# Applying the rms factor of an even block where its projections are read, with the first projection in halves

## What is computed

```python
def rmsnorm(x, g):
    y = xf * lax.rsqrt(jnp.mean(xf * xf, axis=-1, keepdims=True) + EPS)
    return (y * g).astype(x.dtype)

def even_mixer(h, w_in, lb, hg_norm_g, ret_norm_g, w_out):      # h = rmsnorm(x, g[0])
    p = (h @ w_in).astype(jnp.float32)
    hq, hf, hi, hgate, rq, rk, rv, rgate = jnp.split(p, splits, axis=-1)
    f = lb + (1.0 - lb) * jax.nn.sigmoid(hf)
    o_hg = hgrn2_scan(silu(hq), 1.0 - f, jnp.log(f), hi)        # in chunks, 4 heads
    o_hg = head_rmsnorm(o_hg, hg_norm_g) * jax.nn.silu(hgate)
    o_ret = retention_scan(rope(rq), rope(rk) * RET_DK ** -0.5, rv)
    o_ret = head_rmsnorm(o_ret, ret_norm_g) * jax.nn.silu(rgate)
    return jnp.concatenate([o_hg, o_ret], axis=-1) @ w_out
```

## Time and profile before

| | us |
|---|---|
| median of 3 runs | 902.26 |
| lowest, highest | 902.0, 903.86 |
| the profiled execution, its whole time | 902.16 |
| its span, from the first to the last instruction | 900.4 |

### The profile page before, as it was taken

How to read it: one execution, slowest core, us unless ns; L and a number is a source line. 1 busy time by engine, 2 the same in 40 slices (tenths; PEclk the granted TensorE clock), 3 DMA queues, 4 the chain that set the end, 5 groups by cost and what they waited for, 6 DMA issues and landing times.

```text
span 900.4 us, 13334 instructions
## 1 busy us (share of the span) xinstructions
PE 888.8 (99%) x5612; PEld 757.2 (84%) x5612; DVE 650.0 (72%) x789; ACT 498.8 (55%) x671; POOL 31.2 (3%) x25
## 2 busy tenths in 40 slices
PE   9999999999999999999999999999999999999997
PEld 6989888888888888798888888888778998887885
DVE  6898746569777777689576977777668795556655
ACT  7865456465444453756567444445557783356624
POOL 0000000000000000000000000000000083000000
PEclk9999999999999999999999999999999999999999
DMA  9744444366666664544346566666336344234331
GB/s 361 266 142 151 177 140 140 140 236 214 242 231 241 229 242 165 206 146 146 135 141 253 216 243 228 242 243 234 141 127 226 139 141 142 99 112 149 138 135 47
DMA packets 24156, 165.40 MB, mean 184 GB/s; under 512 B 2689, under 2 KB 2945, under 8 KB 4897
## 3 DMA queue, kind: packets, MB, share of 16 engines
q1 hardware_dynamic: 22608, 159.73, 49.3%
q0 software_dynamic: 1056, 4.34, 1.3%
q10 hardware_dynamic: 432, 0.49, 0.2%
HBM read 163.50 MB, written 1.05 MB: 183 GB/s over the span
## 4 chain that ended last, share of the span: by engine, by line
PE 92%; ACT 3%; DVE 3%; DMA 1%; issue 1%; DVEq 0%; ACTq 0%
PE acc L627 29%; PE lin L588 11%; PE lin L609 7%; PE lin L616 7%; PE lin L610 7%; PE lin L593 6%; PE lin L575 3%; PE lin L567 3%; PE lin L568 3%; PE acc L836 1%; DVE w_lo L1859 1%; ACT w_hi L1363 1%; PE acc L719 1%; PE acc L720 1%; PE acc L729 1%; PE lin L672 1%
## 5 line engine op out<-in xcount | busy, mean ns | idle before, releaser
L1859 DVE TENSOR_TENSOR w_lo<-raw,w_hi 128x2048 fp32r<-128x2048 f32 x137 | 318.9, 2338 | 130.8 <-ACT w_hi L1363 130.0
L1363 ACT CAST w_hi<-raw 128x2048 fp32r<-128x2048 f32 x137 | 260.3, 1907 | 148.3 <-DMA raw<-in_weights 92.7
L627 PE MATMUL acc<-w_hi,f_hi 128*128 128x512 f32 x288 | 113.3, 393 | 0.4 <-issue 0.4
L627 PE MATMUL acc<-w_hi,f_lo 128*128 128x512 f32 x288 | 112.3, 390 | 0.0
L609 PE MATMUL lin<-w_hi,h_both 128*128 128x512 f32 x272 | 109.3, 402 | 0.1
L588 PE MATMUL lin<-h_both,w_hi 128*128 128x512 f32 x448 | 106.7, 390 | 0.0
L610 PE MATMUL lin<-w_hi,h_both 128*128 128x512 f32 x272 | 106.3, 391 | 0.0
L588 PEld LDWEIGHTS lin<-h_both,w_hi 128*128 128x128 f32 x448 | 83.2, 188 | 16.7
L627 PE MATMUL acc<-w_lo,f_hi 128*128 128x512 f32 x288 | 79.1, 390 | 0.3 <-DVE w_lo L1859 0.3
L616 PE MATMUL lin<-w_lo,h_both 128*128 128x512 f32 x272 | 68.0, 390 | 0.2 <-DVE w_lo L1859 0.2
L567 PE MATMUL lin<-h_both,w_hi 128*128 128x256 f32 x272 | 67.2, 287 | 0.4 <-ACT arena L1579 0.4
(11 more groups left out here) (368 smaller groups left out, 1224.6 us busy)
## 6 DMA issues: line engine op xcount, KB each, us to landing
raw<-in_weights SPq DMA_DIRECT2D x149, 1024.0 KB, 4.8
rowbuf<-in_rows POOLq DMA_DIRECT2D x6, 512.0 KB, 4.0
x<-in_x_in SPq DMA_DIRECT2D x2, 512.0 KB, 4.4
raw<-in_weights SPq DMA_DIRECT2D x2, 512.0 KB, 6.9
arena<-in_const_even POOLq DMA_DIRECT2D x1, 1024.0 KB, 11.7
out<-x SPq DMA_DIRECT2D x3, 256.0 KB, 2.1
cst<-in_const SPq DMA_DIRECT2D x1, 580.0 KB, 8.2
out<-x ACTq DMA_DIRECT2D x1, 256.0 KB, 2.1
```

What stands on the lines that cost most here:

```text
L627: return pe.matmul(acc[:, at:at + 512], part_of(2 * j + k)[i][:, t * P:(t + 1) * P], w[:, k * 1024 + c * 512:k * 1024 + (c + 1) * 512], st ...
L1363: act.copy(w_hi[:, o % SPLIT, :], raw[:, j % RAW, :]).then_inc(hi_done, 1)
L1859: dve.tensor_tensor(w_lo[:, j % RAW, :], r, hi.bitcast(F32), ALU.subtract).then_inc(tile_split, 1)
```

## The change

- **x without its factor.** PE turns x itself into `acc` as it lands. ACT makes h_hi and DVE h_lo of it without the factor. ACT's squares and root and DVE's reciprocal (`x_r`) come behind tile 1's cast and split. The scaled copy of x is gone.
- **Where the factor is applied.** For feature-major results a row of factors over all partitions is needed: PE turns the two columns of factors (`first_r`, inside the second half of hf), DVE copies them (`every`). hf is then multiplied by it on DVE and goes through ACT's sigmoid in place; hq is multiplied on DVE and goes through ACT's silu in place; for rq and rk the tables of cos and sin are multiplied once. Token-major results are read by ACT with the factor as its scale, in two instructions, one for each 128 tokens, in place of one.
- **The first projection in halves.** Tile 0's high half is cast between h_hi's two halves, and PE goes through chunks 0 to 3 in all three products, then through 4 to 7.
- **The logarithm** is taken before hq is read, and DVE's scan and differences stand ahead of hq's multiply.
- Fewer matmuls that feed no result (8, 2, 7 in place of 16, 4, 6), and `cst` is loaded behind tile 1.

```diff
-                for c in range(2):
-                    after(xn_ready)
...
+                pe.wait_ge(x_loaded[t], 16)
+                for k in range(DC):
+                    mm = pe.transpose(acc[:, k * T + t * P:k * T + (t + 1) * P], x[:, t, k * P:(k + 1) * P], ident)
...
+            def first_r():
+                after(x_r, 2)
+                for t in range(TT):
+                    mm = column_as_row(acc[:, 1024 + t * P:1024 + (t + 1) * P], 10 + t)
+                mm.then_inc(x_r_turned, 1)
...
                 after(z_ready)
                 if l == 0:
-                    read_out(pe, "hq")
+                    after(qs_ready)
...
-            project_feature_major("hf", (1,))
+            project_feature_major("hf", (1,), first_r)
...
             ahead("hf")
-            filled(act, "hf")
-            act.activation(ev("Z0"), pair("hf")[:, :], ACT.Sigmoid).then_inc(freed("hf"), 1)
-            ahead("hq")
-            filled(act, "hq")
-            act.activation(ev("qs"), pair("hq")[:, :], ACT.Silu).then_inc(freed("hq"), 1)
+            read_out(act, "hf")
+            act.activation(ev("Z0"), ev("Z0"), ACT.Sigmoid).then_inc(z0_ready, 1)
+            split_until(LAST["hq"] + 2)
             after(f_gate_ready)
             act.activation(ev("D"), ev("Z0"), ACT.Ln).then_inc(logf_ready, 1)
+            ahead("hq")
+            read_out(act, "hq")
+            act.activation(ev("qs"), ev("qs"), ACT.Silu).then_inc(qs_ready, 1)
...
+            after(x_r_turned)
+            link(dve.tensor_copy(ev("rv", T), acc[:, 1024:1024 + T]))
+            filled(dve, "hf")
+            dve.tensor_tensor(by_head(ev("Z0")), by_head(pair("hf")[:, :]), every, ALU.mult).then_inc(freed("hf"), 1)
+            after(z0_ready)
...
-            ahead("hq")
+            split_until(LAST["hq"] + 2)
             after(logf_ready)
...
             diffs(1)
-            read_out(dve, "hq")
+            turns = by_head(arena[:, E_AT["even"] + CE_AT["cos"][0]:E_AT["even"] + CE_AT["sin"][1]])
+            dve.tensor_tensor(turns, turns, every, ALU.mult).then_inc(turns_ready, 1)
+            ahead("hq")
+            filled(dve, "hq")
+            dve.tensor_tensor(by_head(ev("qs")), by_head(pair("hq")[:, :]), every, ALU.mult).then_inc(freed("hq"), 1)
+            after(qs_ready)
```

More of the change, by code:

```diff
@@ L322, in build @@
         x_turned = sem("x_turned")
+        x_r = sem("x_r")
+        x_r_turned = sem("x_r_turned")
+        z0_ready = sem("z0_ready")
+        qs_ready = sem("qs_ready")
+        turns_ready = sem("turns_ready")
         h_lo_done = sem("h_lo_done")
@@ L891, in first_projection @@
                 open_pair(name)
[L892 to L896, removed]
-                        for b in range(2):
-                            pe.matmul(pair(name)[:, b * T:(b + 1) * T], hi[:, k * 256 + b * P:k * 256 + (b + 1) * P], part[:, k, :],
-                                      start=part is h_hi and b == 0 and k == 0, stop=False)
@@ L900, in first_projection @@
[L900 to L906, removed]
-                mm.then_inc(tile_used, 1)
+                for half in range(2):
+                    ks = range(4 * half, 4 * half + 4)
+                    if half == 0:
+                        pe.wait_ge(first_hi, 1)
+                    else:
+                        high_tile(0)
+                    for part, done in ((h_hi, ht_hi), (h_lo, h_lo_done)):
+                        for k in ks:
+                            if k % 2 == 0:
+                                after(done)
+                            for b in range(2):
+                                w = slice(k * 256 + b * P, k * 256 + (b + 1) * P)
+                                pe.matmul(pair(name)[:, b * T:(b + 1) * T], w_hi[:, 0, w], part[:, k, :],
+                                          start=part is h_hi and b == 0 and k == 0, stop=False)
+                    if half == 0:
+                        pe.wait_ge(first_lo, 1)
+                    else:
+                        low_tile(0)
+                    for k in ks:
+                        for b in range(2):
+                            w = slice(k * 256 + b * P, k * 256 + (b + 1) * P)
+                            mm = pe.matmul(pair(name)[:, b * T:(b + 1) * T], w_lo[:, 0, w], h_hi[:, k, :], start=False,
+                                           stop=k == DC - 1 and b == 1)
@@ L1530, in _, with first_high @@
             act.activation(stat[:, 159:160], stat[:, 158:159], ACT.Sqrt)
+            def first_high(ks):
+                for k in ks:
+                    if k % 2 == 0:
+                        after(x_turned)
+                    ins = act.activation(h_hi[:, k, :], acc[:, k * T:(k + 1) * T], ACT.Identity, scale=col("n0g", k), bias=0.0)
+                    if k % 2 == 1:
+                        ins.then_inc(ht_hi, 1)
+            act.wait_ge(s_small, 16)
+            first_high(range(4))
+            act.wait_ge(first_loaded, 16)
+            act.copy(w_hi[:, 0, 0:1024], raw[:, 0, 0:1024]).then_inc(first_hi, 1)
+            first_high(range(4, 8))
+            act.wait_ge(loaded[0], 16)
+            act.copy(w_hi[:, 0, 1024:2048], raw[:, 0, 1024:2048]).then_inc(hi_done, 1)
+            split_next[0] = 1
+            split_until(2)
             for t in range(TT):
@@ L1535, in _ @@
                 tile_root(t)
[L1536 to L1548, removed]
             def gate_weights(name):
@@ L1583, in half_of, with scaled_out, by_token @@
                 return ev(name, 2048).rearrange("p (t c) -> p t c", t=TT)[:, :, j * 512:(j + 1) * 512]
+            def scaled_out(name, dst, func=ACT.Copy):
+                ahead(name)
+                filled(act, name)
+                for t in range(TT):
+                    ins = act.activation(dst[:, t, :], pair(name)[:, t * 512:(t + 1) * 512], func, scale=r_of(t))
+                ins.then_inc(freed(name), 1)
+            def by_token(ap):
+                return ap.rearrange("p (t c) -> p t c", t=TT)
+            after(x_r, 2)
             split_until(8)
@@ L1593, in _ @@
             level_exp()
-            copy_out("hg", ev("ghg"), ACT.Silu)
+            scaled_out("hg", by_token(ev("ghg")), ACT.Silu)
             split_until(12)
@@ L1616, in _ @@
             act.wait_ge(rope_ready, 2)
-            copy_out("rg0", half_of("gret", 0), ACT.Silu)
+            scaled_out("rg0", half_of("gret", 0), ACT.Silu)
             split_until(22)
@@ L1622, in _ @@
             to_h(["y0b"], y_gain, first=0)
-            copy_out("rg1", half_of("gret", 1), ACT.Silu)
+            scaled_out("rg1", half_of("gret", 1), ACT.Silu)
             split_until(24)
@@ L2019, in first_low, with first_h_low @@
                 return dve.tensor_tensor(w_lo[:, 0, w], raw[:, 0, w], w_hi[:, 0, w].bitcast(F32), ALU.subtract)
+            def first_h_low(ks):
+                for k in ks:
+                    if k % 2 == 0:
+                        after(ht_hi)
+                    ins = dve.scalar_tensor_tensor(h_lo[:, k, :], acc[:, k * T:(k + 1) * T], col("n0g", k), h_hi[:, k, :].bitcast(F32),
+                                                   ALU.mult, ALU.subtract)
+                    if k % 2 == 1:
+                        ins.then_inc(h_lo_done, 1)
+            dve.wait_ge(s_small, 16)
+            first_h_low(range(4))
             after(first_hi)
             first_low(0).then_inc(first_lo, 1)
[L2023 to L2030, removed]
+            first_h_low(range(4, 8))
             dve.wait_ge(hi_done, 1)
@@ L2034, in _ @@
             split_until(2)
+            for t in range(TT):
+                after(ss_ready)
+                after_squares(t)
+                after(sd_ready)
+                dve.reciprocal(stat[:, 10 + t:11 + t], stat[:, 32 + t:33 + t]).then_inc(x_r, 1)
             def gate_weights(name):
```

36 lines of the change are left out of this document (12 added, 24 removed).

## The result

| | before | changed |
|---|---|---|
| median, us | 902.13 (4 runs) | 912.16 (4 runs) |
| lowest, highest | 901.96, 903.86 | 911.44, 913.54 |
| profiled execution, its span | 902.16, 900.4 | 913.54, 911.7 |

The ratio is 1.0105, with a 95% interval of 1.0086 to 1.0124: the changed kernel is about 10 us slower. The direction is the one forecast. The median lies 2 us above the forecast time and 0.16 above the upper end of the range.

What follows compares the result with a forecast made beforehand. It took the matmul engine PE, 99% busy, as the bound. To 902.16 us it added 6.1 for the later start of level 0's scores and 1.9 for the fallen clock, giving 910.2, range 907.5 to 912.

Steps and rivals of the forecast that it cites:

- The bound, and where to look: Whole span: PE is busy 99%, so the start of the first level's scores decides; nothing behind them changes PE's time.
- PE's arrival: Ahead of level 0's scores: PE, turning raw x, would arrive at 38.9, 1.95 us earlier than 40.83.
- DVE's list: DVE's steps from tile 4's split to hq's multiply, then silu at 46.85: scores start at 46.95, 6.1 us later.
- tile 4's ends at 28.45: DVE's split of tile 4, start of its queue: ends at 28.45; POOL's earlier constants may delay the tile by up to 0.7.
- The clock: Behind PE's 8 us wait at level 0: TensorE's clock falls, costing 1.9 us, bounds 0 and 3.
- a short stop costs no clock: PE's 1.48 us stop ending at 379.81: eight turns behind it take 1.07 us, read as no fall of the clock.
- The clock that stays up: Rival: same wait at level 0, but TensorE's clock does not fall; 908.3 us, chance 30%.
- The late start: Rival: x is turned at the low clock level at the kernel's start, tile 4 late besides; 911.8 us, chance 8%.
- That the gain survives: Rival: DVE delivers hq's multiply by 37.8, so qs is there when PE comes; 900.2 us, chance 4%.

Runs made afterwards that it cites:

- third experiment: Changed kernel with POOL's constants (mask, cos, sin, decay, first row) waiting for tile 4 instead of tile 1: 910.35 us, ratio 1.0084.
- second experiment: Changed kernel with 38 matmuls of 512 columns that feed no result, ahead of level 0's scores on PE: 909.42 us, ratio 1.0082.
- first experiment: Changed kernel with hq's multiply on DVE moved ahead of the scan, right behind the split of tile 5: 906.36 us, ratio 1.0045.

## Why the prediction came out as it did

- **The bound, and where to look.** Right: apart from level 0 and the clock, PE's waits are those of before, and behind level 1 the shift stays between 9.8 and 10.1 us up to the second fall of the clock.
- **PE's arrival.** 38.9 was worked out and 39.0 measured, in part by luck, since two misses cancel. PE began half 1 of hf 2.3 us sooner than before (15.62 against 17.92) and not 2.8. The stop for the factors and their two turns then took some 0.4 us and not 0.85. hq began 1.9 us sooner (21.80 against 23.68), as forecast.
- **DVE's list.** The mechanism and each step were right. From the copy's start to silu's end the list gave 18.4 us, the trace 18.2 (29.56 to 47.77). The term that was mis-sized is the start of the list, "tile 4's ends at 28.45": it ended at 29.56, since tile 4 landed at 25.4. I had named the reason, POOL's earlier transfers, bounded it at 0.7 and then put 0 into the sum; it was 1.2 at the landing and 1.1 in the split. The third experiment, in which POOL waits, takes 1.0 of it back. With it the scores start at 47.91 and not 46.95.
- **The clock.** That it falls was right, and the second experiment shows both the cause and the size. The price was mis-sized: 1.9 by the nine slow matmuls of the start, 2.7 measured. The sum took the work at the low level to be as long as at the kernel's start, 3.7 us from the first matmul at 1.20 to 4.90 (the column of the granted clock shows 1.00 there; it is the 0.43 us from one matmul to the next that tell the level); behind the wait it lasted 5.8. My upper bound of 3 held it.
- **The sum.** 8.0 forecast, 10.0 by the medians: 1.0 from tile 4 and 0.8 from the clock. The rest, about 0.2, is not resolved by four executions. The second fall of the clock, worth 1.5 us in the profiled one, is in no term of the sum; the step that left it out is the sentence "a short stop costs no clock", read from one execution in which it had not.
- **The range.** The median lies 0.16 above its end of 912. The forecast's own terms at their upper bounds (6.1, 0.3, 0.7 and 3 on 902.16) add up to 912.3, so the range was closed tighter than they allow; and the bound of 0.7 on tile 4 was itself too small.
- **The rivals.** The clock that stays up is refuted by the windows. The late start, whose 911.8 lies nearest to the median, did not happen: PE arrived at 39.0. Only the late tile 4 in it was true. That the gain survives needed splits and scan to overtake each other in DVE's queue, which they cannot do by themselves; written in another order they can, and then the gain was there (0.9982). The prediction's 93% for slower was for the order as it stood.

The Trainium skill ("TensorE: Matmul & The Clock Gate", "What's actually happening") says that an idle array returns to half rate. The windows of the changed kernel agree, with 0.50 from 46 to 53 after the wait of 8.9 us.

## What to carry to other kernels

An instruction that is put into the queue of an engine with 30% idle time is not free: ask at which place it stands, what it is queued behind, and which engine's next work hangs on it; here a multiply of 1.2 us behind the scan held PE for 8.9 us, and ahead of it for 1.6. When the start of a critical engine is pulled forward, write down the arrival of each operand it meets afterwards, because the first one that did not move takes the whole gain. And a wait of the matmul engine can cost more than its length, since the work behind it may run at the low clock for a while, here 1.5 to 2.7 us behind waits of 2.4 to 8.9. Matmuls that feed no result, inside an unavoidable wait, kept the clock up behind the 8.9 us wait and gave back 2.7 us; for a stop of 1.5 us no run shows clearly that they pay.

## What the hardware showed that I had not expected

- **Short stops can be followed by a fall of the clock.** In the changed kernel's profiled execution it fell 1.7 us after PE had resumed from a stop of 1.5 us (0.50 from 392 to 395); in the kernel before's it did not fall there (rows 9). In the first experiment it fell 0.9 us after a stop of 2.4 us, and not behind the one of 1.6 us ahead of it. If it varies from execution to execution, as these two of the same stop suggest, it would explain much of the spread of the kernel before; that is not shown.
- **The price of a fall varies, and not with the length of the wait.** The work done at the low level was 5.7 us behind a wait of 3.8 (cost 2.7 us), 5.8 behind one of 8.9 (2.7), some 3.2 behind one of 7.8 (1.5), and 3.7 at the kernel's start. The runs do not show what sets it.
- **Transfers that start earlier delay others.** POOL's constants, issued 1.4 us sooner, and one place's move of `cst` left SP's fifth tile 1.2 us later; holding POOL back moved it 3.4 us forward.
